# Roots of head norms spread over VectorE's queue, and gate tiles that take their PSUM banks from four

## What is computed

```python
def first_block(x, mem, ...):
    for l in range(2):
        x = x + hybrid_mixer(rms_norm(x, norm_mix[l]), ...)     # neighbourhood attention and grouped-query attention
        x = x + memory_cross_attention(...)
        x = x + conv_ffn(...)
    return rms_norm(x, norm_final)

def second_block(x, ...):
    for i in range(2):
        x = x + 0.5 * swiglu(...)
        z, xbc, dt_raw, q, k, v = split(rms_norm_2(x, mix_norm[i]) @ w_in[i])
        xbc = silu(causal_depthwise_conv(xbc, conv_w[i], conv_b[i]))
        y_ssd = ssd_mixer(xbc, dt_raw, z, ...)                   # gated by silu(z)
        q, k = rms_norm_2(q, q_norm[i]), rms_norm_2(k, k_norm[i])  # per head
        x = x + concat([y_ssd, dilated_attention(q, k, v)]) @ w_out[i]
        x = x + 0.5 * swiglu(...)
    return x
```

## Time and profile before

| | |
|---|---|
| median of 3 runs | 1887.54 us (1887.22 to 1887.64) |
| profiled execution, device time | 1887.55 us |
| its span, first to last instruction | 1885.8 us |
| busy: PE, DVE, ACT, POOL | 1878.2, 1451.7, 1170.4, 397.5 us |
| granted TensorE clock, mean of the span | 1.000 of 2.4 GHz |

### The profile page before, as it was taken

The page is one execution under the profiler, slowest core; times in us unless marked ns, Lnnn a source line. Parts: engine busy times, 40 slices in busy tenths (PEclk is TensorE's granted clock), DMA queues, the critical chain, the costliest instruction groups (busy, mean ns, idle before and its releaser), DMA issues.

```text
span 1885.8 us, 29598 instructions
## 1 busy us (share of the span) xinstructions
PE 1878.2 (100%) x11164; PEld 1628.2 (86%) x11164; DVE 1451.7 (77%) x2607; ACT 1170.4 (62%) x2165; POOL 397.5 (21%) x456
## 2 busy tenths in 40 slices
PE   9999999999999999999999999999999999999999
PEld 8889988897898888888988788888888898878887
DVE  6877996677799769866787978757885687897874
ACT  6667785567678556545667565545554667756552
POOL 2210211011011005411022214402440102223430
PEclk9999999999999999999999999999999999999999
DMA  9344566543465656665554355555555544445553
GB/s 354 124 141 145 194 204 204 173 152 123 136 196 192 206 170 205 190 195 180 179 167 136 124 189 190 190 191 186 192 190 191 189 158 153 150 145 185 189 193 127
DMA packets 92333, 334.62 MB, mean 177 GB/s; under 512 B 10240, under 2 KB 10784, under 8 KB 91808
## 3 DMA queue, kind: packets, MB, share of 16 engines
q1 hardware_dynamic: 92192, 332.73, 53.6%
HBM read 331.61 MB, written 1.08 MB: 176 GB/s over the span
## 4 chain that ended last, share of the span: by engine, by line
PE 91%; DVE 6%; ACT 2%; issue 1%; DVEq 0%; ACTq 0%
PE PS L83 88%; PE PS L86 3%; DVE WL L98 2%; DVE TMP L98 1%; DVE TMP L108 1%; DVE TMP L105 1%; ACT TMP L95 1%; ACT WH L92 1%; DVE SM L114 1%; DVE M L108 0%; DVE SM L108 0%; ACT TMP L92 0%; ACT M L92 0%; ACT TMP L94 0%; DVE SM L105 0%
## 5 line engine op out<-in xcount | busy, mean ns | idle before, releaser
L98 DVE TENSOR_TENSOR WL<-RAW,WH 128x1024 fp32r<-128x1024 f32 (+1 forms) x610 | 760.1, 1251 | 281.5 <-ACT WH L92 277.8
L92 ACT ACTIVATE WH<-RAW 128x1024 fp32r<-128x1024 f32 (+1 forms) x610 | 640.1, 1053 | 310.0 <-PE PS L83 305.3
L83 PE MATMUL PS<-WH,GX 128*128 128x512 f32 (+1 forms) x1636 | 524.7, 392 | 0.0
L83 PE MATMUL PS<-HX,WH 128*128 128x512 f32 (+1 forms) x1920 | 523.5, 344 | 0.4
L83 PE MATMUL PS<-HX,WL 128*128 128x256 f32 x1488 | 413.9, 281 | 0.0
L83 PE MATMUL PS<-GX,WH 128*128 128x256 f32 (+1 forms) x1776 | 409.6, 330 | 0.4
L83 PEld LDWEIGHTS PS<-HX,WH 128*128 128x128 f32 x1920 | 331.1, 189 | 46.6 <-DVE TMP L108 0.8
L83 PEld LDWEIGHTS PS<-WH,GX 128*128 128x128 f32 x1636 | 306.2, 188 | 64.6 <-issue 3.7
L83 PEld LDWEIGHTS PS<-GX,WH 128*128 128x128 f32 x1776 | 298.0, 190 | 30.2 <-DVE TMP L108 0.8
L83 PE MATMUL PS<-WL,GX 128*128 128x512 f32 (+1 forms) x818 | 317.1, 388 | 0.0
L98 POOL TENSOR_TENSOR TMP<-TMP,RB 128x256 f32<-128x256 f32 x176 | 205.6, 1172 | 473.5 <-DVE TMP L98 235.1
(11 more groups left out here) (146 smaller groups left out, 1679.4 us busy)
## 6 DMA issues: line engine op xcount, KB each, us to landing
RAW<-wts SPq DMA_DIRECT2D x607, 512.0 KB, 4.3
CUM<-rows SPq DMA_DIRECT2D x8, 512.0 KB, 4.9
M<-bias SPq DMA_DIRECT2D x4, 320.0 KB, 11.7
M<-bias SPq DMA_DIRECT2D x1, 1280.0 KB, 8.8
X<-x SPq DMA_DIRECT2D x2, 512.0 KB, 10.9
M<-mem SPq DMA_DIRECT2D x1, 1024.0 KB, 13.0
M<-memt SPq DMA_DIRECT2D x1, 1024.0 KB, 11.4
CST<-cst SPq DMA_DIRECT2D x1, 794.0 KB, 12.6
```

Source lines behind the costliest of these rows:

```text
L83: return Issued(self.eng and self.eng.matmul(o, l, r, start=first, stop=last, skip_group_check=share))
L92: return Issued(self.eng.activation(o, i, f, scale=scale))
L98: return Issued(self.eng and self.eng.tensor_tensor(o, a, b, op))
```

## The change

1. **Gate tiles and cb.** z(2) to z(7), and cb(0) to cb(3), may all take any of the banks 0, 1, 2, 7. Before, z had 0, 1, 2 and cb had 7.
2. **Roots of block 1.** `newton` becomes a generator `newton_steps`. The keys' roots (4 columns) are taken by `key_scales` one small instruction at a time, between DVE's work on memory activations, WL tiles and the rotation of the queries. The queries' roots (16 columns) follow in `query_scales`, with one WL tile put between its third and fourth instruction. Instead of 19 instructions there are 32 in each layer.
3. **Roots of block 2.** The 17 instructions of `scales` stand between WL tiles and taps of n = 10 and n = 11. The keys' scales are written first, and POOL waits for these alone before it scales the first raw keys.

```diff
-                        fm_tile(("z", L, m), whole, WT if m >= 2 else (0, 1))
+                        fm_tile(("z", L, m), whole, WT + STB if m >= 2 else (0, 1))
...
-                        ps = take(("cb", L, g), STB)
+                        ps = take(("cb", L, g), WT + STB)
...
                     for n in range(4):
                         lows((("gq", L), 2 * n + 1))
+                        if n:
+                            next(of_keys)
                         yield
                         if n == 0:
                             rotate_keys()
+                            of_keys = key_scales()
                         if n < 2:
                             memory(2 * n + 4)
+                            next(of_keys)
                             memory(2 * n + 5)
+                            next(of_keys)
                     lows(("mk", L, 0))
-                    rotate_queries(0)
+                    next(of_keys)
+                    rotate_queries(0, of_keys)
                     yield
                     lows(("mk", L, 1))
-                    rotate_queries(1)
-                    rotated_scales()
+                    next(of_keys)
+                    rotate_queries(1, of_keys)
+                    run(of_keys)
+                    of_queries = query_scales()
+                    for _ in range(3):
+                        next(of_queries)
                     lows(("mk", L, 2))
+                    run(of_queries)
                     lows(("mk", L, 3))
...
                 for n in range(16):
+                    if n == 10:
+                        of_heads = scales(L)
+                        next(of_heads)
                     lows(("xbc", L, n))
+                    next(of_heads, None)
                     lows((("qk", L, 2 + n // 8), n % 8))
-                    behind(n)
+                    next(of_heads, None)
+                    behind(n, of_heads)
+                    next(of_heads, None)
...
-                    if n == 10:
-                        scales(L)
                     if n == 11:
+                        for _ in of_heads:
+                            pass
                         dt_sums()
...
-                e.wait_ge(small, ("scl", L, 0))
                 for b in (1, 0, 2):
+                    e.wait_ge(small, ("scl", L, "keys" if b == 1 else 0))
```

More of the change, by code:

```diff
@@ L2080, in block1, with rotate @@
                 rms_columns()
-                def rotate(out, tmp, src, cos, sin, heads, key):
+                def rotate(out, tmp, src, cos, sin, heads, key, aside=iter(())):
                     def by_half(a, h):
@@ L2087, in rotate @@
                          cos.unsqueeze(1).to_broadcast([128, heads, 64]), ALU.mult).then_inc(made)
+                    next(aside, None)
                     e.wait_ge(added)
@@ L2109, in rotate_queries, with key_scales @@
                     e.total(SUMS1[:, t, 0:8], rot_sq(t).rearrange("p (h d) -> p h d", h=8)).then_inc(added)
-                    rotate(rot_q(t), rot_sq(t), bank(key)[:, :], QC[:, t, :], QS[:, t, :], 8, key)
+                    next(aside, None)
+                    rotate(rot_q(t), rot_sq(t), bank(key)[:, :], QC[:, t, :], QS[:, t, :], 8, key, aside)
                     e.tt(rot_q(t), rot_q(t), rot_sq(t), ALU.add).then_inc(made, ("gq", L, t))
-                def rotated_scales():
+                    next(aside, None)
+                def key_scales():
                     e.wait_ge(added)
                     e.wait_ge(small)
-                    v3 = smc(0, 20).rearrange("p (t n) -> p t n", t=2)
+                    v3, y3 = (smc(o, 4).rearrange("p (t n) -> p t n", t=2) for o in (0, 160))
                     for t in range(2):
-                        e.ts(v3[:, t, :], SUMS1[:, t, :], RXC2[:, t:t + 1], EPS, ALU.mult, ALU.add).then_inc(small)
-                    y3 = newton(20).rearrange("p (t n) -> p t n", t=2)
+                        e.ts(v3[:, t, :], SUMS1[:, t, 8:10], RXC2[:, t:t + 1], EPS, ALU.mult, ALU.add).then_inc(small)
+                        yield
+                    yield from newton_steps(4)
                     for t in range(2):
-                        e.ts(SCQ[:, t, 0:8], y3[:, t, 0:8], RXC[:, t:t + 1], 0.125, ALU.mult, ALU.mult).then_inc(small)
-                        e.ts(SCQ[:, t, 8:10], y3[:, t, 8:10], RXC[:, t:t + 1], None, ALU.mult).then_inc(
-                            small, ("scq", L))
+                        e.ts(SCQ[:, t, 8:10], y3[:, t, :], RXC[:, t:t + 1], None, ALU.mult).then_inc(small)
+                        yield
                     e.wait_ge(small)
-                    e.wait_ge(made)
+                    e.wait_ge(made, ("rotated k", L))
                     for t in range(2):
@@ L2130, in rotated_scales, with query_scales @@
                     m.then_inc(made, ("gk", L))
+                def query_scales():
+                    e.wait_ge(added)
+                    e.wait_ge(small)
+                    v3, y3 = (smc(o, 16).rearrange("p (t n) -> p t n", t=2) for o in (0, 160))
+                    for t in range(2):
+                        e.ts(v3[:, t, :], SUMS1[:, t, 0:8], RXC2[:, t:t + 1], EPS, ALU.mult, ALU.add).then_inc(small)
+                        yield
+                    yield from newton_steps(16)
+                    for t in range(2):
+                        e.ts(SCQ[:, t, 0:8], y3[:, t, :], RXC[:, t:t + 1], 0.125, ALU.mult, ALU.mult).then_inc(
+                            small, ("scq", L))
                 def memory(k):
@@ L2439, in taps @@
                     for d in (1, 2, 3):
+                        if d > 1:
+                            next(aside, None)
                         e.wait_ge(made)
@@ L2445, in taps, with behind @@
                             i.then_inc(made, ("taps", L, m), key)
-                def behind(n):
+                def behind(n, aside=iter(())):
                     if 2 <= n <= 17:
-                        taps(n - 2)
+                        taps(n - 2, aside)
                 def sums(b):
@@ L2642, in scales @@
                 e.wait_ge(small)
-                v3 = smc(0, 48).rearrange("p (t n) -> p t n", t=2)
+                v3, y3 = (smc(o, 48).rearrange("p (t n) -> p t n", t=2) for o in (0, 160))
                 for t in range(2):
                     e.ts(v3[:, t, :], SUMS[:, t, 0:24], RX2[:, t:t + 1], EPS, ALU.mult, ALU.add).then_inc(small)
-                y3 = newton(48).rearrange("p (t n) -> p t n", t=2)
+                yield
+                yield from newton_steps(48)
                 for t in range(2):
-                    e.ts(SCL[:, t, 0:8], y3[:, t, 0:8], RX[:, t:t + 1], 0.125, ALU.mult, ALU.mult).then_inc(small)
                     e.ts(SCL[:, t, 8:24], y3[:, t, 8:24], RX[:, t:t + 1], None, ALU.mult).then_inc(
+                        small, ("scl", L, "keys"))
+                for t in range(2):
+                    e.ts(SCL[:, t, 0:8], y3[:, t, 0:8], RX[:, t:t + 1], 0.125, ALU.mult, ALU.mult).then_inc(
                         small, ("scl", L, 0))
```

20 lines of the change are left out of this document (15 added, 5 removed).

## The result

| | before | after |
|---|---|---|
| median, first comparison | 1887.55 us (1887.22 to 1887.64, 4 runs) | 1938.04 us (1937.10 to 1940.40, 4 runs) |
| profiled execution | 1887.55 us | 1940.40 us |
| its span | 1885.8 us | 1938.6 us |
| mean granted clock | 1.000 | 0.988 |

The ratio is 1.027 (95% interval 1.0257 to 1.0282): the changed kernel is slower by 50.5 us. The forecast was 1948, with a range of 1922 to 1960. So the direction, the range and the mechanism held, and the time was forecast 10 us too high. The changed kernel's runs lie 3.3 us apart, those of before 0.4. One of the 11 executions of e4 further down ran at a granted clock of 0.753 and took 2297.36 us; it is left out of the comparisons.

A forecast was written before the change was run, and what follows sets the result against it. PE was taken to bound the kernel, carrying 91% of the chain that ended last. Waits 38.4 plus half clock 23.0, less 0.4 and 0.6 for the roots, gave 60.4 on 1887.55: 1948 us, range 1922 to 1960.

The forecast's parts named there:

- The gate tiles' waits: z(2) to z(5) wait for the fold two tiles before: 19.18 us a layer, 38.4 us lost in all.
- the fold of z(0) owes nothing to PE: Nothing leading to this fold waits for z(2), so it does not move and z(2) starts 5.65 us later.
- the later ones hang on the turn behind the delayed tile: Folds after z(0)'s follow the turn behind the late tile: z(3), z(4) lose 5.27 us each, z(5) 2.99.
- The rival in which the folds catch up: DVE and ACT idle while PE waits, so folds come half a stop sooner: 1900 to 1915 us; chance 0.07.
- The clock: Eight stops each bring PE's clock to half, one following gate tile slow: 2.87 us a stop, 23 us in all.
- The rival in which the clock stays up: Clock needs more than a stop between bursts to fall, so only the waits remain: 1925 us; chance 0.16.
- The roots of block 1: Keys' turn, layer 0, wins 0.86 us, layer 1 nothing; net gain 0.4, from 0.9 gain to 1.5 loss.
- up to 0.5 given back at the scores behind it: In layer 0 DVE's first maximum starts late, about 85.6 instead of 84.97, costing PE up to 0.5 us.
- The roots of block 2: taps(9) end about 2 us sooner, so PE's gaps of 0.29 and 0.31 us at xbc(13) go: 0.6 us won.
- What a spread root step costs: Each small root step standing between DVE's other work takes about 0.10 us, bounds 0.08 and 0.13.

The follow-up runs named there:

- e4: Kernel before with spread roots, its own bank sets, and DVE folding z(m-1) right behind the WL of step m: median 1885.28 us, ratio 0.9989.
- e9: Changed kernel with 11 unread float32 matmuls ahead of z(2), z(3), z(4) and 6 ahead of z(5), keeping PE at work: 1923.89 us.
- e1: Changed kernel with the bank sets of before; the spread roots of blocks 1 and 2 stay: 1885.92 us, ratio 0.9992 to before.
- e3: Changed kernel, banks as changed, with DVE folding z(m-1) behind the WL of step m, one iteration earlier: 1886.01 us, ratio 0.9993 to before.
- e6: Changed kernel with DVE's fold of z(m-2) ahead of the WL in the same iteration instead of behind it: 1920.74 us, ratio 1.0176 to before.
- e2: Kernel before with one line changed: cb may take banks 0, 1, 2, 7; gate tiles keep 0, 1, 2: 1940.23 us, ratio 1.028.
- e8: Kernel before with only the roots of block 2 spread and POOL's wait for the keys' scales: 1886.76 us, ratio 0.9996.
- e5: Changed kernel with 22 unread float32 matmuls ahead of z(2), z(3), z(4) and 12 ahead of z(5); the filling outlasted the wait: 1953.11 us.
- e10: The changed kernel run once more, unaltered, on the same chip as the run with PE kept at work in its stops: 1938.96 us.

## Why the prediction was right, and where it was off

**The gate tiles' waits.** Forecast 38.4 us, measured 38.0 (e9 against e1). Stop by stop 5.65, 5.27, 5.27 and 2.99 were forecast, and 5.64, 5.11, 5.11 and 2.99 came (3.36 less the 0.37 that was there). The working held: the fold of z(0) owes nothing to PE, the later ones hang on the turn behind the delayed tile, and 0.47 us lie between fold and matmul. The 0.16 us too much at z(3) and z(4) are mostly one step, from ACT's copy of the probabilities to the first exponentials: 0.51 us were taken and 0.39 came (1031.68 to 1032.07 in the changed kernel). e3 and e6 show that it is the fold's place and nothing else that PE waits for; e2 shows that the set of cb does it. The rival in which the folds catch up fell, and its premise that DVE and ACT idle while PE waits was wrong. They work while PE waits (DVE for 4.62 and ACT for 3.67 us of the 5.70 from 1016.80 to 1022.50) and idle while PE is at the gate tile, for what they need next comes from PE behind that tile.

**The clock.** This term was mis-sized: 23 us forecast, 15.1 measured. Two steps of it failed. First, a matmul of 256 columns was taken to double from 0.12 to 0.24 us, and so a slow tile to cost 2.87 us; the step goes to 0.213, and z(2), all of it at the lower level, took 5.41 us against 3.05 in e9: 2.36 more, which makes 18.9 for eight. Second, not every tile ran wholly at the lower level: the stretches say 0.50, 0.65, 0.63 and 0.57. By their lengths above the eight tiles lost 15.8 us in the profiled execution, and what stands behind them another 0.9. The fourth stop is the plainest case. The stop ahead of z(5) from the turns on, and two stretches of its tile, in the changed kernel:

```profile
1056.70:1061.40 4.70, 1.65 (x12) 1.24 (x10) 2.53 (x4) 2.58 (x5) 0.00 (x0) 1.00 0.00 0
1061.46:1063.20 1.74, 1.74 (x13) 1.74 (x14) 0.00 (x0) 0.00 (x0) 0.00 (x0) 0.90 0.57 165
1063.30:1066.00 2.70, 2.70 (x14) 2.48 (x15) 0.00 (x0) 0.00 (x0) 0.00 (x0) 0.50 0.20 79
```

The clock was at the upper level all through the stop, the tile began at it, and it fell to the lower one while PE was at work. From the end of before's trace, where the clock fell some 2 us behind PE's last matmul, I had read that every stop of 3 us or more has it down when its tile begins. This stop shows otherwise: it can fall later. In layer 1 the clock also came back before a slow tile had ended (z(2) of that layer: 1.00 from 1650.30 to 1651.40). The rival in which the clock stays up (1925) is what e9 makes by force, 1923.89, so its sum was right and its premise false.
Of this the Trainium skill (TensorE: Matmul & The Clock Gate, HAM oscillation) says that PE's waits between bursts bring the half clock back, and that the next burst starts at it. This case agrees in that each of the eight stops was paid, 15.1 us in all. It differs at z(5) of layer 0, which began at 1.00 and fell on the way.

**The roots of block 1.** Forecast a net gain of 0.4 us, with 0.86 won at the turn and up to 0.5 given back at the scores behind it. The turn was won as forecast, 0.86, and 0.11 more at its twin in layer 1, where nothing was expected. The loss, 0.4 us, came at another place and 3 us earlier, and left 0.6 net. The view by tile (GX, 78 to 79.5) names what ended PE's 0.3 us ahead of 78.58:

```profile
  DVE SQ L98: 0.3, 1
```

That is the last read of the tile of queries in PSUM, whose bank PE wants. In the changed kernel's timeline of DVE it stands at

```profile
77.05 0.68 DVE L98 TENSOR_TENSOR TMP<-PS,SM 128x512 f32<-128x512 f32 x1
77.65 0.22 DVE L104 TENSOR_SCALAR SM<-SM 128x2 f32<-128x2 f32 x1
77.78 0.74 DVE L98 TENSOR_TENSOR SQ<-PS,SM 128x256 f32<-128x256 f32 x2
```

1.0 us later than the same row before (`SQ` at 76.77), behind the keys' root steps. The step that failed is mine: I named who waits for the scaled keys, but not who waits for the other work that these instructions were put in front of. At the scores nothing was lost: the first maximum starts at 85.00 (84.97 in the earlier trace rows, 85.6 forecast), and PE's steps show no loss there.

**The roots of block 2.** 0.6 us forecast, 0.6 measured (e8, by the medians; 0.8 by the steps, as the matmul behind each xbc(13) gap had been late too). POOL's first instruction came at 955.15 instead of 955.68. Since PE is 0.9 us earlier there, that is 0.4 us later against PE, where I had expected one; it had cover either way.

**What a spread root step costs.** The forecast took 0.10 us for each, between 0.08 and 0.13. DVE of e1, the first ones in layer 0:

```profile
66.29 0.23 DVE L105 TENSOR_SCALAR SM<-SM 128x2 f32<-128x2 f32 x1
66.42 1.22 DVE L98 TENSOR_TENSOR WL<-RAW,WH 128x1024 fp32r<-128x1024 f32 x1
67.56 0.17 DVE L104 TENSOR_SCALAR SM<-SM 128x4 int32<-128x4 int32 x1
67.63 0.49 DVE L108 SCALAR_TENSOR_TENSOR GX<-M,CST,GX 128x256 fp32r<-128x256 f32 x1
```

The next operation starts 0.07 us behind the start of a root step (67.56 to 67.63), 0.13 behind the first one of the chain (66.29 to 66.42), against 0.21 between dependent steps in the earlier trace rows. So taking a chain of small dependent operations apart does pay, by two thirds of its length. The Trainium skill (VectorE: DVE Perf Modes, The DRAIN you can't avoid) says of eight `tensor_copy` in a row that a semaphore between them costs nothing extra. For operations as small as these the rows differ from that: a step that waits for the one before starts 0.21 us behind it, one that doesn't 0.13 or 0.07, and the measurement decides.

## What to carry to other kernels

When buffers are given out to whoever's turn it is, letting a short-lived tile into the set of the long-lived ones can take a buffer from these even when the union of the sets is larger. Count, for each long-lived tile, the distance to its predecessor in the same buffer, and set it against the place of the instruction that frees that buffer. The cheapest repair may be that place: here an operation of 0.41 us, issued one iteration earlier in its queue (five times a layer), undid a loss of 52 us.

A stop of a few microseconds on TensorE can cost more than itself: 1.9 us on top of 4.75 here, on average, with a tile of 3 us behind each. A stop of 0.75 us (e6) cost nothing beyond itself. Before a chain is spread between other work, look at who waits for the work that it is put in front of, and not only for the end of the chain.

## What was not expected of the hardware

- The granted clock can fall behind a stop, when the engine is at work again (z(5) of layer 0: 1.00 through the stop, 0.90 for the stretch up to 1063.20, then 0.50). It stayed at 1.00 behind the stops of 0.75 us in e6.
- At the lower level a matmul of 256 columns takes 0.213 us from start to start and 0.12 at the upper: 1.8 times, not twice.
- A matmul of 256 columns with float32 operands takes 0.43 us and leaves two records (e5, e9); one of the split products, whose operands are float32r, takes 0.12.
- What the lower clock costs differs between executions with the same order and the same waits: 13.7, 16.5 and 16.8 us in the traces of e2, e10 and the changed kernel.
